# A gate projection's last two blocks moved into the attention steps, a one-queue prologue and a scan mask in PSUM

## What is computed

```
c_act = jax.nn.silu(c)
mod = (c_act @ mod_w[i] + mod_b[i])[:, None, :]
sh1, sc1, gt1, sh2, sc2, gt2 = jnp.split(mod, N_MOD, axis=-1)
h = modulate(rms_norm(x, norm_mix_g[i]), sh1, sc1)     # h * (1 + scale) + shift
xx = token_shift(h) - h
xr, xw, xk, xv, xa, xg = (h + xx * mu[j] for j in range(6))
```

```
w_log = -jax.nn.softplus(-(w0 + jnp.tanh(xw @ w1) @ w2)) - 0.5
decay = jnp.exp(-jnp.exp(w_log.astype(jnp.float32)))
```

```
qg = h @ w_qg
q, gate = qg[..., :D_MODEL], qg[..., D_MODEL:]
q = rms_norm(split_heads(q), q_gain).transpose(0, 2, 1, 3)
s = jnp.einsum('bhqd,bhkd->bhqk', qb, k) * sm_scale + Fq[..., :, None] - F[..., None, :]
s = jnp.where(kpos[None, :] <= qpos[:, None], s, -jnp.inf)
o = jnp.einsum('bhqk,bhkd->bhqd', jax.nn.softmax(s, axis=-1), v)
return (o * jax.nn.sigmoid(gate)) @ w_o
```

## Time and profile before

| | us |
|---|---|
| runs before | 2559.11, 2554.51, 2558.77; median 2558.77 |
| profiled execution | 2556.14 |
| its span | 2554.4 |
| PE busy | 2457.1 (96%) |
| POOL busy | 1524.4 (60%) |
| DVE busy | 1253.9 (49%) |
| ACT busy | 742.8 (29%) |

### The profile page before, as it was taken

The page is one execution under the profiler, slowest core; times in us unless marked ns, Lnnn a source line. Parts: engine busy times, 40 slices in busy tenths (PEclk is TensorE's granted clock), DMA queues, the critical chain, the costliest instruction groups (busy, mean ns, idle before and its releaser), DMA issues. The chain is left out here.

```text
span 2554.4 us, 36315 instructions
## 1 busy us (share of the span) xinstructions
PE 2457.1 (96%) x14692; PEld 1930.0 (76%) x14692; DVE 1253.9 (49%) x1853; ACT 742.8 (29%) x1440; POOL 1524.4 (60%) x772
## 2 busy tenths in 40 slices
PE   5999988999999999999999999999999999999998
PEld 4767676788888777667888877888775478787886
DVE  7737347775562254443544426876485643121212
ACT  5744433331120212543311212333324431111210
POOL 4784726677777676116988883533262067754774
PEclk9999999999999999999999999999999999999999
DMA  7322426566552232103656532333344273311221
GB/s 283 107 83 75 117 84 261 230 239 223 226 220 95 91 107 86 53 2 144 231 214 223 204 116 95 117 116 116 142 144 149 101 295 133 113 66 67 82 99 66
DMA packets 89901, 358.81 MB, mean 140 GB/s; under 512 B 27288, under 2 KB 41112, under 8 KB 52384
## 3 DMA queue, kind: packets, MB, share of 16 engines
q1 hardware_dynamic: 64992, 227.69, 24.8%
q10 hardware_dynamic: 24768, 129.12, 13.3%
HBM read 317.70 MB, written 39.06 MB: 140 GB/s over the span
## 5 line engine op out<-in xcount | busy, mean ns | idle before, releaser
L530 POOL TENSOR_TENSOR whi<-wraw,con_sb 128x512 fp32r<-128x512 f32 (+1 forms) x305 | 625.7, 2071 | 831.4 <-PE ps L586 611.3
L534 POOL TENSOR_TENSOR wlo<-wraw,whi 128x512 fp32r<-128x512 f32 (+1 forms) x305 | 796.1, 2630 | 12.8
L586 PE MATMUL ps<-hh,whi 128*128 128x512 f32 x936 | 365.7, 391 | 0.0
L586 PE MATMUL ps<-hh,wlo 128*128 128x512 f32 x936 | 364.3, 389 | 0.0
L586 PE MATMUL ps<-hl,whi 128*128 128x512 f32 x936 | 364.2, 389 | 0.0
L586 PEld LDWEIGHTS ps<-hh,whi 128*128 128x128 f32 x936 | 175.7, 188 | 41.0 <-issue 4.6
L586 PEld LDWEIGHTS ps<-hh,wlo 128*128 128x128 f32 x936 | 175.7, 188 | 36.6
L586 PEld LDWEIGHTS ps<-hl,whi 128*128 128x128 f32 x936 | 175.8, 188 | 36.0
L586 PE MATMUL ps<-midh,whi 128*128 128x512 f32 x512 | 199.7, 390 | 0.0
L586 PE MATMUL ps<-midh,wlo 128*128 128x512 f32 x512 | 199.2, 389 | 0.0
L586 PE MATMUL ps<-midl,whi 128*128 128x512 f32 x512 | 199.2, 389 | 0.0
(11 more groups left out here) (511 smaller groups left out, 4622.1 us busy)
## 6 DMA issues: line engine op xcount, KB each, us to landing
wraw<-wst SPq DMA_DIRECT2D x162, 1024.0 KB, 4.8
cond_w<-wcond ACTq DMA_DIRECT2D x68, 1024.0 KB, 4.8
first_w<-wcond SPq DMA_DIRECT2D x8, 1024.0 KB, 19.6
mod_w<-wcond SPq DMA_DIRECT2D x8, 1024.0 KB, 13.5
d_v<-key_and_query ACTq DMA_DIRECT2D x4, 1536.0 KB, 5.4
d_s<-ssb ACTq DMA_DIRECT2D x4, 1536.0 KB, 5.2
sld<-d_s SPq DMA_DIRECT2D x4, 1536.0 KB, 7.0
vld<-d_v SPq DMA_DIRECT2D x16, 384.0 KB, 3.4
```

The source lines that it names most:

```text
L530: o = pool.tensor_tensor(whi[:, s, c], wraw[:, f, c], C("zero").broadcast_to([P, width]), ALU.add)
L534: o = pool.tensor_tensor(wlo[:, s, c], wraw[:, f, c], whi[:, s, c].bitcast(F32), ALU.subtract)
L586: o = e.matmul(ps[:, b, :nt], w[:, k, mc], x[:, k0 + k, t0:t0 + nt], start=first and k == 0 and j == 0, stop=final and k == nk - 1 and j == 2)
```

## The change

The kernel after has three edits in one.

**Prologue.** All loads but one row are on SP's queue, in the order: the first 258 columns of `con` (identity, ones, two constants), x in four pieces, the eight `first_w`, one block of weights, the vectors, the rest of `con`, the second block. ACT's queue loads one row of 4 KB, which TensorE copies to all partitions by two fp32 matmuls with one row of ones; SiLU goes from PSUM to PSUM. POOL adds the squares in pairs, so that TensorE sums four tiles, not eight. The reciprocal root moves between DVE's third and fourth dot product, and POOL multiplies x by the spread root. `gains` and `stay` (two small DVE operations) move into this stage. In the next one `scale` is gone; the shift is ACT's for even tiles and DVE's for odd ones.

**Mask.** ACT copies the mask to a PSUM bank behind its read-outs of `cum`, and the scans read it from there.

**Gate.** Blocks q0+6 and q0+7 are left out ahead of the attention. `late_gate` issues their 96 matmuls into bank 7 during the first 24 steps, four a step: 1, 2 and 1 at three places of a step, or all four at its end where s is a multiple of 6. ACT makes exp(−g) of a finished tile and DVE the rest of the sigmoid in pieces. Values, spread and scale share bank 6, so that `spread_sums` waits for `gate`, and `scale` for `weigh`; spread, weigh, part and the halves of `scale` move by a step or so. `scale(0, ·)` moves from behind j = 6 into the middle of block j = 5. `ptr` has two buffers instead of four, one of them the space of the key weights, so that `load_key(3)` moves from before the attention to behind it.

```diff
-                sp.dma_start(vec[:], A["vec"]).then_inc(*SP.up16(sem("vec_loaded")))
-                sp.dma_start(con[:], A["con"]).then_inc(*SP.up16(sem("con_loaded")))
+                sp.dma_start(con[:, :early], A["con"][:, :early]).then_inc(*SP.up16(sem("con_loaded")))
+                for j in range(4):
+                    sp.dma_start(x_sb[:, 2 * j:2 * j + 2], A["xT"][:, 2 * j:2 * j + 2]).then_inc(*x_in[j].dma())
...
+                pool.wait_ge(*root_laid.at(1))
+                for k in range(KT):
+                    pool.tensor_tensor(x_sb[:, k], x_sb[:, k], root_rows[:], ALU.mult).then_inc(*x_normed.inc())
...
-                act.dma_start(first_row[:], A["crow"][0]).then_inc(*row_in.dma())
-                act.dma_start(x_sb[:], A["xT"]).then_inc(*AC.up16(sem("x_loaded")))
+                act.dma_start(first_row[:], A["crow"][0, 0:1]).then_inc(*row_in.dma())
+                act.wait_ge(*row_laid.at(1))
+                act.activation(row_at, row_at, ACT.Silu).then_inc(*row_ready.inc())
...
+                for n in range(2):
+                    o = pe.matmul(ps[:, 4 + n], ones[0:1], first_row[:, T * n:T * n + T], start=True, stop=True)
...
-                inverse_root(dve, rooted, inverted)
+                        if (n, m) == (1, 0):
+                            inverse_root(dve, rooted, inverted)
...
-                def scale(k):
-                    dve.scalar_tensor_tensor(x_sb[:, k], x_sb[:, k], coef[:, 0, k:k + 1], ps[:, 7], ALU.mult,
-                                             ALU.mult).then_inc(*scaled.inc())
+                def shift(k):
+                    dve.tensor_scalar(hpad[:, k, 1:], x_sb[:, k], coef[:, 0, k:k + 1], mod[0][:, k:k + 1], ALU.mult,
+                                      ALU.add).then_inc(*shifted_odd.inc())
...
-                    dve.tensor_tensor_scan(cum[:, g], C("keep"), cum[:, g], 0.0, ALU.mult, ALU.add).then_inc(*scanned.inc())
+                    dve.tensor_tensor_scan(cum[:, g], mask_at, cum[:, g], 0.0, ALU.mult, ALU.add).then_inc(*scanned.inc())
...
+                act.wait_ge(*mix_ready.at(before_scans))
+                act.activation(mask_at, C("keep"), ACT.Copy).then_inc(*mask_laid.inc())
...
+                def late_gate(first, n):
+
+                    for at in range(first, first + n):
...
+                        if step_ == 0:
+                            turn["begun"] = max(turn["begun"], q + 1)
+                            pe.wait_ge(w_split, q + 1)
+                            if tile_ > EARLY:
+                                pe.wait_ge(*late_read.at(tile_ - EARLY))
+                        o = pe.matmul(ps[:, GATE], w[:, k, P * m:P * m + P], x[:, k], start=step_ == 0, stop=step_ == 3 * KT - 1)
...
-                for j in range(1, 8):
-                    block_of(pe, q0 + j, 0, hh, hl, KT, 256, bank_free=bank_free)
-                    if j <= 4:
-                        length_sums(j <= 2, (j - 1) % 2)
-                    if j == 6:
+                for j in range(1, 6):
+                    if j == 5:
+                        block_of(pe, q0 + j, 0, hh, hl, KT, 256, mn=1, bank_free=bank_free)
                         pe.wait_ge(*rows_made.at(3))
                         scale(0, 0)
                         scale(0, 1)
+                        block_of(pe, q0 + j, 0, hh, hl, KT, 256, m0=1, mn=1, tell=False, bank_free=bank_free)
...
                 for s in range(NS):
                     i, t = s // 4, s % 4
+                    opening = s % 6 == 0
                     if s + 1 < NS:
                         scores(s + 1)
+                    if t == 1 and i:
+                        spread_sums(i - 1)
+                    if not opening:
+                        fill(1)
+                    if t == 0 and i:
+                        values(i - 1)
+                    turn_p(2 * s)
+                    if t == 2 and i + 1 < KT:
+                        scale(i + 1, 1)
+                    if not opening:
+                        fill(2)
+                    turn_p(2 * s + 1)
                     if t == 1 and i + 1 < KT:
                         scale(i + 1, 0)
-                        scale(i + 1, 1)
-                    turn(2 * s)
-                    turn(2 * s + 1)
-                    if t == 0 and i:
-                        values(i - 1)
-                        spread_sums(i - 1)
+                    fill(4 if opening else 1)
...
-                fold_read_out(act, 11, 4)
+                fold_read_out(act, 11, 4, key_free=False)
```

More of the change, by code:

```diff
@@ L174, in constants @@
     c["ones"] = np.ones((P, P))
+    c["epsn"] = np.full((P, 1), NORM_EPS)
+    c["zero"] = np.zeros((P, 1))
     c["head"] = same * 1.0
@@ L823, in turned_read_out @@
                 act.dma_start(d_fold[h], fold_out[:].rearrange("p m c -> p (m c)")).then_inc(fold_stored, 16)
+        small_sb = tiles("small_sb", 73, shape=[P, T])
+        stay, one_ka = small_sb[:, :6 * KT], small_sb[:, 192:192 + KT]
         x_sb = tiles("x", 0, KT)
@@ L869, in _ @@
                 pe.wait_ge(sem("con_loaded"), 16)
-                for k in range(KT):
-                    square_sum(pe, k, squared, summed)
+                pe.wait_ge(*row_in.at(16))
+                for n in range(2):
+                    o = pe.matmul(ps[:, 4 + n], ones[0:1], first_row[:, T * n:T * n + T], start=True, stop=True)
+                o.then_inc(*row_laid.inc())
+                for j in range(4):
+                    pe.wait_ge(*paired.at(j + 1))
+                    for t in range(4):
+                        o = pe.matmul(ps[:, 7, t:t + 1], sq[:, 2 * (j % 2), P * t:P * t + P], ones[:, 0:1],
+                                      start=j == 0 and t == 0, stop=j == 3, skip_group_check=True)
+                    o.then_inc(*summed.inc())
                 spread_root(pe, inverted, spread)
@@ L1078, in decay @@
                     dve.tensor_tensor(ax, ps[:, 5], en[:, g % 2], ALU.mult).then_inc(*decayed.inc())
[L1079 to L1084, removed]
+                shift(1)
                 for n in range(KT):
                     mixing(n)
-                    if n + 3 < KT:
-                        scale(n + 3)
+                    if n % 2 == 0 and n + 3 < KT:
+                        shift(n + 3)
                     if n:
@@ L2473, in program @@
         otile = tiles("otile", 25, shape=[P, T])
-        pr, ptr = tiles("pr", 64, 4), [tiles(f"ptr{b}", 8 + 4 * b, 4) for b in range(4)]
+        pr, ptr = tiles("pr", 64, 4), [key_w, tiles("ptr1", 70, 4)]
+        EARLY = KT // 2
         oh, ol = tiles("oh", 48, KT, F32R), tiles("ol", 32, KT, F32R)
@@ L2534, in scale @@
                 def scale(i, j):
-                    if i >= 2:
-                        pe.wait_ge(*(gated if j else weighted).at(i - 1))
+                    if i >= 2 and j == 0:
+                        pe.wait_ge(*weighted.at(i - 1))
                     elif i:
-                        pe.wait_ge(*pair_normed.at(j + 1))
-                    pe.matmul(ps[:, VALUES if j else SPREAD], pair_rows[:, i], rms_split[:, j], start=True,
+                        pe.wait_ge(*pair_normed.at(2 * i + j))
+                    pe.matmul(ps[:, scale_bank(i, j)], pair_rows[:, i], rms_split[:, j], start=True,
                               stop=True).then_inc(*gain_spread.inc())
@@ L2693, in _ @@
                 root_of(0)
-                for k in range(KT):
+                for k in range(EARLY):
                     read_g(k)
-                fold_read_out(act, 11, 4)
+                fold_read_out(act, 11, 4, key_free=False)
                 exp(0)
@@ L2699, in _ @@
                 for n in range(NI):
+                    if n % 12 == 0 and 0 < n <= 12 * EARLY:
+                        j = n // 12 - 1
+                        act.wait_ge(*late_made.at(j + 1))
+                        act.activation(g_sb[:, EARLY + j], ps[:, GATE], ACT.Exp, scale=-1.0).then_inc(*late_read.inc())
                     copy(n)
@@ L2783, in _ @@
                         gate(i - 1)
+                    if t == 1 and i:
                         weigh(i - 1)
[L2785 to L2787 removed]
+                    if t == 2 and i + 1 < KT:
+                        norm(i + 1, 1)
+                    if t == 3 and i:
                         part(i - 1)
+                    late_inverse(s)
                 sum_inverse_of(KT - 1)
```

156 lines of the change are left out of this document (109 added, 47 removed).

## The result

The changed kernel takes 2560.09 us, median of 20 runs (2552.99 to 2567.13), against 2555.28 us for the kernel before (20 runs, 2550.68 to 2559.11): a ratio of 1.0018, 95% interval 1.0012 to 1.0025. It is slower by about 4.8 us, within the 0.2% that the prediction called the same, but to the other side of the small gain that it forecast. (The median of three on which the prediction's 2558 stood was 3.5 us above that of twenty.) The profiled execution took 2561.13 us with a span of 2559.3, 5.0 us more than the profiled one before, so the two traces show the whole difference.

A forecast was written before the change was run, and what follows sets the result against it. TensorE, busy 96% of the span, was taken as the bound. Prologue −2.5, mask −3.0 and gate +4.7 sum to −0.8 us, giving 2558 against a median of 2558.77; own range 2553 to 2563, over all cases 2549.5 to 2566.

The forecast's parts named there:

- A: Prologue: earlier weights and a shorter second block bring the first projection matmul forward, −2.5 us (−4 to 0).
- B: Decay scans: mask in PSUM frees POOL, removing TensorE's 1.98 us wait and the half clock behind it, −3.0 us (−3.6 to 0).
- R3: Prologue and scans: POOL isn't released, the root chain eats the gain, both parts give nothing; 2563 to 2564, chance 0.10.
- C (a): Ahead of the attention: four gate tiles of 24 matmuls removed, −21.7 us.
- (b): Block j=5: TensorE waits at `scale(0, ·)` for a DVE operation held by POOL, +4.3 us, and a clock fall behind, +1.0.
- C (c): Attention's start: with the key load moved behind, the first exponential comes some 1.3 us earlier; −2.2 us (−2.9 to 0).
- C (d): Attention: sixteen filler matmuls in each of six pairs, 3.4 us for five pairs and 3.6 for pair 0, +20.6 (18 to 26).
- R1: Attention: fillers ride in gaps, 0.2 us a step hidden, so the kernel is faster, 2552; chance 0.28.
- R2: Attention: each filler group costs a drain beside turn matmuls, 64 groups at 0.09 us, 2564, or 2569 at both sides; chance 0.16.
- C (e): Attention: longer chain in pairs 6 and 7, +2.0 us (0 to 3); late sigmoid's first DVE operation held by POOL, +0.7 (0 to 3).
- The longer chain: Attention pairs 6 and 7, without fillers: spread and norm wait through one shared bank, +2.0 us (0 to 3).
- C: The gate's part: matmuls moved from ahead of the attention into it, with stops and fillers, +4.7 us in all.

The follow-up runs named there:

- the run with both mends: The changed kernel with `scale(0, ·)` behind block j=5 and DVE's part of the late sigmoid two steps later: 2550.88 us, ratio 0.9982 to the kernel before.
- the run with the first stop mended: The changed kernel with `scale(0, ·)` behind block j=5 instead of in its middle, nothing else: 2554.08 us, ratio 0.9992 to the kernel before.

## Why the prediction was wrong

Step by step, forecast against the two traces.

- **A** was −2.5 and is −2.2 by the trace, 0.9992 alone. DVE's first product starts at 12.94 instead of 11.4, DVE waited 2.17 for the root instead of 3 to 5, and its products ended at 33.6 against 34.0. The second block's start takes 4.2 us (34.52 to 38.68) against the 4.6 that I worked out. Not foreseen: of the 3.83 that the first matmul is earlier, 1.6 is given back in waits for mixed tiles and for POOL's split, which a later TensorE didn't meet.
- **B** was −3.0 and is −3.8, in each step as written: POOL's pieces at 4.0, no wait, no 0.50 behind it. The later scans cost nothing. R3 falls with A and B.
- **C (a), (b)**: (a) is as forecast. The stop at `scale(0, 0)` was foreseen with its engine and operation and cost 5.8 instead of 5.3, by the clock behind it (1.7 instead of 1.0).
- **C (c)** was −2.2 and is −3.4, of which the load is 0.6 to 0.7 instead of 1.3 and 2.7 is a half clock in the one trace that I took for the kernel before. That the term came out on the good side is luck. Pair 0 with its twelve fillers takes 11.57 us.
- **C (d)** was 3.4 a pair and is 3.5 (15.86 − 12.33), right in size and not in its reasons, which is luck too. That the attention has 0.4 us a pair to give away was read from busy records whose ends are modelled: the turns gave up 1.7 when fillers stood between them. That there is no price between equal shapes was wrong as well: twelve groups cost 1.3, about 0.1 each. So R1 and R2 each named something real, and the two cancel; neither forecast of the time came true.
- **C (e)** holds the step that failed. For the late sigmoid's operation I wrote +0.7 with 0 to 3 as bounds. It was held as long as L2713, which I had as the pattern, and pairs 3 and 4 lost 3.6. Its meeting with the split is no chance: the split of `fo`'s first block is released by the first filler of the gate's last block, at the end of step 12, and the operation stands in step 13; all four traces with this order have it. I had the release rule and the step number, and took a mean where the order decides. The longer chain was +2.0 and is 2.1: 1.1 in pair 6 and 1.0 from there to the last spread.
- **Outside the sum**: 1.2 us at 187 and 1.7 at 1190, both half clock in the trace after and not before. No edit stands at 187: the run with prologue and mask alone has this fall too (a granted clock of 0.81 from 181 to 189), the run with both mends hasn't. Near 1190 the key's load is the nearest edit; the mask alone, without it, has the fall, and the run with the first stop mended, with it, hasn't.

So the forecast of C, +4.7, was 3.0 too low: 2.9 of the second stop, 0.6 of the fillers, 0.1 of the chain, 0.5 of the first stop, less 1.1 of pair 0. With A and B 0.6 better than forecast and 2.9 outside the sum that leads from −0.8 to the +5.0 of the two traces, within half a microsecond. Either the second stop or what lies outside the sum was enough to turn the sign of −0.8. The first was a term given its value between two bounds without asking which of the two cases the program's order makes true; the cause of the second, half clock at two places, no run shows.

That a DVE operation is held as long as POOL's is in line with the Trainium skill, page SBUF — State Buffer, section "Who interferes with whom": a DVE operation with two SBUF inputs contends with a POOL operation that reads SBUF, one in a two-port mode, which `tensor_scalar` can enter, contends with POOL too, and there the one that issues first has the shared ports for its whole instruction. The trace agrees with 4.90 beside 4.71 and 4.76 beside 4.56, POOL's starting first both times, and with 0.42 once they are apart. In which mode the `tensor_scalar` ran no row says.

## What to carry to other kernels

When work is moved, list each DVE operation that a bottleneck engine will now wait for, and ask what POOL is doing at that step: which semaphore releases it, and by which instruction of the new order. Here a two-step shift of an operation of 0.42 us was worth 3.6 us, and a stop that the order shows is better moved behind columns that have to be done anyway. Spreading matmuls into a stage that is itself full of them moved time here and made none: a pair grew by 3.5 us for fillers of 3.62 by columns. Before a wait or a clock fall in one trace is put down to an edit, look at the same place in a run that doesn't touch it: here that took 2.7 us from the key's load.

## What the runs showed of the hardware

A scan of 512 columns with its multiplier in PSUM takes 1.20 us and holds up no POOL operation; with the multiplier in SBUF it took up to 1.99, and POOL's four pieces 7.37 instead of 4.04.

Half clock came at different places in different executions of the same instructions. Behind a wait of 1.56 us for the first exponential pair 0 ran at 0.72 in the trace before, and behind one of 1.59 at 1.00 with the mask alone. In the recurrence from 290 to 400 us TensorE waits for nothing that the profile names ("issue") for 7.8 us before, 8.2 after, 6.4 with both mends and 11.1 with the key's load moved, with the same instructions there; the lead or lag of a trace against before moves there by up to 6 us. So two single executions can't be compared by their ends to better than that, which is why the totals were read from medians and the causes from the stretch where an edit stands.
